# Reordering the setup of a two-layer decoder trunk, and computing the two coarsest tree levels of its decay scores as small tiles

## The chip, the core and the metric

The kernel runs on one core of a Trainium2 chip. The metric is the device time of one execution in microseconds. The kernel was run three times, and the median of the runs is what a change is judged by. One further execution was recorded by the hardware profiler, and all rows shown come from that one.

The engines are called by their profile names: PE is TensorE (PEld its weight loads), ACT is ScalarE, DVE is VectorE, POOL is GpSimd, SP is SyncE, which here only issues the weight transfers.

## What is computed

One inference step of a two-layer trunk with 256 prompt tokens and 8 single-token samples, 264 columns in all, with a model width of 1024. Each layer is a feed-forward block, a mixer and a second feed-forward block. Each block is normalised and modulated by a condition vector (adaLN), and all weights are float32. The mixer has three branches: A and C are gated linear recurrences with 4 heads, B is a convolution with a gated scan.

```python
mod = (c @ w_ada[l] + b_ada[l]).reshape(B, N_SUB, 3, D_MODEL)[:, :, :, None, :]
h = ada_norm(x, norm_gain[l, 0], mod[:, 0, 0], mod[:, 0, 1])
x = x + 0.5 * mod[:, 0, 2] * swiglu(h, w_ffn_in[l, 0], w_ffn_out[l, 0])
h = ada_norm(x, norm_gain[l, 1], mod[:, 1, 0], mod[:, 1, 1])
y, sa, scv, sh, sc = mixer_block(h, ...)
x = x + mod[:, 1, 2] * y
h = ada_norm(x, norm_gain[l, 2], mod[:, 2, 0], mod[:, 2, 1])
x = x + 0.5 * mod[:, 2, 2] * swiglu(h, w_ffn_in[l, 1], w_ffn_out[l, 1])
```

The recurrence of A and C is, per token, S_t = diag(f_t) S_{t-1} + k_t v_t^T and o_t = S_t^T q_t. Written out for the prompt it needs a score for each pair of a query token t and a key token s before it: the product of q_t and k_s, weighted by all decays between them.

## The kernel before

**Weight units.** All matmuls of the trunk run in a sequence of units. A unit is 128x1024 weights. SP loads it into one of six buffers of `raw`; ACT rounds it to `whi` (`split_hi`, line 419); DVE takes the difference as `wlo` (`split_lo`, line 427); PE then runs three matmuls per 128x128 block (`mm3`, lines 462 to 464: high by high, high by low, low by high). `whi` and `wlo` have four slots, and both splits are issued three units ahead (`LOOK`). Per layer there are 44 units for a feed-forward input, 24 for its output, and 82 for the mixer.

**Order by hand.** Each engine walks through the units in one loop and does its own part of the other work at unit numbers written in the tables `AT`, `EARLY_AT`, `HEAD_AT`, `PE_LV` and `RG_AT`. Engines run their queues in order, so a step that waits holds up everything placed behind it. The results of a group of matmuls lie in rotating banks; `take_bank` makes PE wait until the group three before has been evacuated, by ACT or DVE (`BY_ACT`). For the mixer's units 46 to 57 the gate tiles `mb` are evacuated by ACT into `sg`, and the two halves of each `br b` unit by DVE.

**Condition blocks.** `c @ w_ada` is done in blocks of eight tiles of 128x1024 (`ada_units`, line 617), which `to_mod` on DVE transposes and adds to the bias. Two blocks are needed before the first unit: block 0, the scale, is tiles 0 to 7, and block 1, the shift, is tiles 8 to 15. Their tiles go to a buffer `first`; PE waits for them in groups of four. Later blocks run at the units of `plan_ada` and `MIX_ADA`.

**Setup.** PE transposes the inputs, takes tiles 0 to 3, transposes the small parameters (`rows`), takes tiles 4 to 7, sums the squares of x (`add_squares`), takes tiles 8 to 11, spreads the root (`spread_root`), takes tiles 12 to 15 and runs ten matmuls that compute nothing (`keep_warm`, two instructions each). ACT squares x, then runs Exp, Exp and Ln for the gate parameters, then the root of the mean square. DVE copies x and the parameters, does some twenty small operations on the parameters and three on masks, then the reciprocal of the root (line 1664), `to_mod(0)`, the eight scaled tiles (line 2128), `split_lo(0)`, `to_mod(1)` and the low parts of the first eight tiles (line 2140). POOL builds seven level masks from DVE's mask operations.

**Decay tree.** The scores are built in nine levels, `LEVELS = [0, 1, 2, 4, 8, 16, 32, 64, 128]`. At level m a key in the first half of a block of 2m tokens meets a query in its second half, and `update` multiplies q and k by the decays so far. `level` on PE multiplies, for each head and each of two 128-token tiles, all 128 keys with the 64 queries that are in second halves (128x128 weights, 64 columns); `keep` on DVE copies from the bank to `sc` only where the level's mask says so (`copy_predicated`). `PE_LV` places the levels; level 32 of A is at unit 38, level 64 at 43; those of C are at 47 and 50. `keep` and `update` follow one unit later.

**Sample states.** POOL's chain for six batches of states: broadcast v (`outer`, line 1086), multiply with k (line 1092, event `kv`), load the next state batch (`st_load`). ACT scales the loaded state (at `AT['st']`), and DVE adds the product (event `st_new`, at `AT['kv']` + 1), which releases the next `outer`. Then PE multiplies with q (`AT['so']`).

## Time and profile before

| what | value |
| --- | --- |
| median of 3 runs | 1497.16 us (1493.77 to 1501.41) |
| the profiled execution | 1495.62 us |
| its span, first to last instruction | 1493.5 us |
| mean granted clock of PE, share of full speed | 0.996 |
| busy: PE, PEld | 1460.4 us (98%), 1393.4 us (93%) |
| busy: DVE, ACT, POOL | 941.7 us (63%), 779.2 us (52%), 108.8 us (7%) |
| HBM traffic | 215 GB/s over the span |

Busy time of an engine is the time in which it ran an instruction; matmuls are pipelined, so a busy PE isn't PE at its peak. A timeline row gives the start and the length in microseconds, the engine, the line, the operation, the output and inputs with their shapes, a count where rows were merged, and in brackets the idle time before it with what ended that. In a chain view, matmuls and their weight loads are counted once for each pass: a float32 matmul of the kinds here is two instructions.

### The profile page before, as it was taken

Reading aid. Unit: us, or ns where it says so; the run is one execution under the profiler, and the core shown is the slowest. Engines: PE = TensorE matmul, PEld = TensorE weight load, DVE = VectorE, ACT = ScalarE, POOL = GpSimd, SP = SyncE. Lnnn points to the kernel's source line nnn. Section 1 sums busy time; section 2 is a strip of 40 time slices with the busy share of each in tenths; the row PEclk is TensorE's granted clock in tenths of the full one; section 3 lists DMA queues with packets and bytes.
Section 4 is the critical chain, followed back from the end, with each engine's and each line's share of the span. In section 5 each row is a group of like instructions: output and inputs, shape, how many; then the busy total and the mean of one; then the engine's idle time right before and its main releaser. Section 6 shows DMA issues by size and latency. Waiting matters only on the chain.

```text
span 1493.5 us, 30844 instructions
## 1 busy us (share of the span) xinstructions
PE 1460.4 (98%) x12902; PEld 1393.4 (93%) x12902; DVE 941.7 (63%) x1579; ACT 779.2 (52%) x1236; POOL 108.8 (7%) x143
## 2 busy tenths in 40 slices
PE   5999999999999999999999999999999999999998
PEld 4999999999988999999999999999999899999997
DVE  4545546778856677555576545577897667855553
ACT  2534435776446566444464444478643555744442
POOL 3000000012120030000000000000122102000000
PEclk9999999999999999999999999999999999999999
DMA  9689897688787755888957789867889856578661
GB/s 340 193 233 260 239 263 207 191 234 241 210 214 220 211 166 164 247 254 241 260 163 226 226 242 270 231 191 214 242 220 248 234 154 193 164 223 227 181 189 40
DMA packets 460026, 323.59 MB, mean 217 GB/s; under 512 B 11219, under 2 KB 435707, under 8 KB 459890
## 3 DMA queue, kind: packets, MB, share of 16 engines
q1 hardware_dynamic: 451952, 299.44, 70.2%
q0 software_dynamic: 6880, 20.41, 4.9%
q8 instruction: 102, 1.67, 0.5%
q10 hardware_dynamic: 1058, 1.79, 0.3%
q14 instruction: 34, 0.28, 0.1%
HBM read 313.29 MB, written 8.37 MB: 215 GB/s over the span
## 4 chain that ended last, share of the span: by engine, by line
PE 89%; issue 3%; DVE 2%; DMA 2%; POOL 1%; ACT 1%; ACTq 1%; DVEq 0%; POOLq 0%
PE bank L462 27%; PE bank L463 26%; PE bank L464 26%; PE bank L617 4%; PE bank L777 2%; DMA st<-in_state_gla 1%; DMA rows<-in_b_ada 1%; ACT st L1155 1%; POOL xA L1092 1%; DVE wlo L427 0%; PE bank L817 0%; ACTq L1164 0%; DMA raw<-in_w_ada 0%; PE bank L629 0%; PE bank L644 0%
## 5 line engine op out<-in xcount | busy, mean ns | idle before, releaser
L427 DVE TENSOR_TENSOR wlo<-raw,whi 128x1024 fp32r<-128x1024 f32 (+1 forms) x436 | 518.5, 1202 | 386.7 <-ACT whi L419 386.5
L462 PE MATMUL bank<-hH,whi 128*128 128x264 f32 x2048 | 588.9, 288 | 1.9 <-DVE hL L2140 1.4
L463 PE MATMUL bank<-hL,whi 128*128 128x264 f32 x2048 | 580.8, 284 | 0.0
L464 PE MATMUL bank<-hH,wlo 128*128 128x264 f32 x2048 | 580.1, 283 | 0.0
L419 ACT ACTIVATE whi<-raw 128x1024 fp32r<-128x1024 f32 (+1 forms) x436 | 444.2, 1034 | 193.0 <-PE bank L464 152.2
L462 PEld LDWEIGHTS bank<-hH,whi 128*128 128x128 f32 x2048 | 385.8, 188 | 19.9 <-issue 16.5
L463 PEld LDWEIGHTS bank<-hL,whi 128*128 128x128 f32 x2048 | 386.2, 189 | 0.0
L464 PEld LDWEIGHTS bank<-hH,wlo 128*128 128x128 f32 x2048 | 384.4, 188 | 0.0
L462 PE MATMUL bank<-hidH,whi 128*128 128x264 f32 x704 | 201.5, 286 | 0.0
L464 PE MATMUL bank<-hidH,wlo 128*128 128x264 f32 x704 | 200.0, 284 | 0.0
L463 PE MATMUL bank<-hidL,whi 128*128 128x264 f32 x704 | 199.5, 283 | 0.0
L462 PEld LDWEIGHTS bank<-hidH,whi 128*128 128x128 f32 x704 | 132.4, 188 | 2.8 <-issue 2.5
L464 PEld LDWEIGHTS bank<-hidH,wlo 128*128 128x128 f32 x704 | 132.7, 188 | 0.0
L463 PEld LDWEIGHTS bank<-hidL,whi 128*128 128x128 f32 x704 | 132.3, 188 | 0.1
L1155 ACT ACTIVATE hidH<-hid 128x264 fp32r<-128x264 f32 x88 | 37.3, 423 | 148.7 <-DVE hid L1541 148.7
L462 PE MATMUL bank<-uH,whi 128*128 128x274 f32 x320 | 94.4, 295 | 0.0
L463 PE MATMUL bank<-uL,whi 128*128 128x274 f32 x320 | 92.8, 290 | 0.0
L464 PE MATMUL bank<-uH,wlo 128*128 128x274 f32 x320 | 92.5, 289 | 0.0
L1155 ACT ACTIVATE sil<-bank 128x264 f32<-128x264 f32 x76 | 29.7, 391 | 103.0 <-PE bank L464 102.9
L462 PE MATMUL bank<-yH,whi 128*128 128x264 f32 x256 | 74.8, 292 | 6.1 <-ACT sg L1155 3.8
L464 PE MATMUL bank<-yH,wlo 128*128 128x264 f32 x256 | 73.2, 286 | 0.0
L463 PE MATMUL bank<-yL,whi 128*128 128x264 f32 x256 | 73.2, 286 | 0.0
(307 smaller groups left out, 1713.9 us busy)
## 6 DMA issues: line engine op xcount, KB each, us to landing
raw<-in_w_ffn_in SPq DMA_DIRECT2D x176, 512.0 KB, 5.5
raw<-in_w_ada SPq DMA_DIRECT2D x128, 512.0 KB, 4.5
raw<-in_w_in SPq DMA_DIRECT2D x120, 512.0 KB, 5.2
raw<-in_w_ffn_out SPq DMA_DIRECT2D x64, 512.0 KB, 6.3
raw<-in_w_ffn_out SPq DMA_DIRECT2D x32, 384.0 KB, 6.1
first<-in_w_ada SPq DMA_DIRECT2D x16, 512.0 KB, 12.1
raw<-in_w_out SPq DMA_DIRECT2D x16, 512.0 KB, 4.9
out<-st POOLq DMA_DIRECT2D x12, 512.0 KB, 4.6
```

Source lines behind the costliest of these rows:

```text
L419: nc.scalar.activation(whi[:, s, 0:w], raw[:, r, 0:w], ACT.Copy).then_inc(hi_done, 1)
L427: nc.vector.tensor_tensor(wlo[:, s, 0:w], raw[:, r, 0:w], whi[:, s, 0:w].bitcast(F), ALU.subtract).then_inc(lo_done, 1)
L462: nc.tensor.matmul(out, a, rh, start=start, stop=False)
L463: nc.tensor.matmul(out, a, rl, start=False, stop=False)
L464: return nc.tensor.matmul(out, b, rh, start=False, stop=stop)
L617: last = mm(ps[32 * j:32 * j + 32, 0:256].rearrange("p (b i) -> p b i", i=32), cst[:, kt], src[:, j], start=(kt == 0), stop=(kt == KT - 1))
L777: last = mm(out, k_, q_, start=True, stop=True)
L1092: g.tensor_tensor(v_, v_, bc(k_, [P, NB, P]), ALU.mult).then_inc(S["kv"], 1)
L1155: return nc.scalar.activation(out, in_, func, **k)
```

## The change

The setup is reordered. PE waits for the first condition tiles in groups of 6, 5, 4 and 1; it takes tiles 0 to 5, the sums of squares, the parameter transposes, tiles 6 and 7, the spread of the root, then tiles 8 to 15. ACT runs one Sqrt on a dummy ahead of the squares and goes to the root without Exp and Ln. These (`small_act`) move to the first feed-forward stage at unit 13, and DVE's small operations to units 12 (`small_start`) and 15 (`small_end`), the mask operations included; DVE copies the parameters behind the reciprocal. The buffer `setup_t` is moved so that it lives that long.

At levels 32 and 64 of the tree PE multiplies only the keys and queries that belong together: 64x64 scores, or two 32x32 ones, per head and tile, written to their own partitions. DVE copies them without a mask.

The first output unit of the mixer waits for the weights of the second one only when it comes to them. Places of single steps change:

| table entry | before | after |
| --- | --- | --- |
| `MIX_ADA`, last of six | 66 | 63 |
| `AT['kv']`, batch 0 | 22 | 20 |
| `AT['st']`, batch 5 | 48 | 49 |
| `EARLY_AT['conv']`, third tile | 15 | 13 |
| `HEAD_AT['A']['scaled']`, first pair | 56 | 55 |
| `HEAD_AT['C']['spread']`, first pair | 64 | 63 |

The diff without these entries; the removed lines of the small operations, cut here, come back in `small_end`:

```diff
@@ -30,6 +30,8 @@
...
 FIRST = 16
+FIRST_GROUPS = (range(0, 6), range(6, 11), range(11, 15), range(15, 16))
+FIRST_OF = {n: i for i, g in enumerate(FIRST_GROUPS) for n in g}
 UW = NT + 10
@@ -47,7 +49,7 @@
...
 
-MIX_ADA = (10, 16, 29, 44, 53, 66)
+MIX_ADA = (10, 16, 29, 44, 53, 63)
 ADA_BLOCKS = [(0, 1), (0, 0)]
@@ -317,7 +319,7 @@
...
         landed = [sem(f"landed{i}") for i in range(RAW)]
-        first_in = [sem(f"first_in{i}") for i in range(FIRST // 4)]
+        first_in = [sem(f"first_in{i}") for i in range(len(FIRST_GROUPS))]
         hi_done = sem("hi_done")
@@ -512,7 +514,7 @@
...
                 if n < FIRST:
-                    sp.dma_start(first[:, n], src).then_inc(first_in[n // 4], 16)
+                    sp.dma_start(first[:, n], src).then_inc(first_in[FIRST_OF[n]], 16)
                 else:
@@ -607,7 +609,7 @@
...
                     if n < FIRST:
-                        pe.wait_ge(first_in[n // 4], 64)
+                        pe.wait_ge(first_in[FIRST_OF[n]], 16 * len(FIRST_GROUPS[FIRST_OF[n]]))
                         tile = first[:, n, :]
@@ -681,7 +683,7 @@
...
                         if (L, f, k) == (0, 0, 0):
-                            pe.wait_ge(set_dve, 3 + KT + 1 + kt + 1)
+                            pe.wait_ge(set_dve, 2 + KT + 1 + kt + 1)
                         elif k == first and kt % 2 == 0:
@@ -771,6 +773,11 @@
...
                         out = AUX[bank][:, col:col + n]
+                        if m in (32, 64):
+                            for c in range(0, P, 2 * m):
+                                last = mm(AUX[bank][c:c + m, col:col + m], K[br][rows_, j, s0 + c:s0 + c + m],
+                                          Q[br][rows_, j, s0 + c + m:s0 + c + 2 * m], start=True, stop=True)
+                            continue
                         if 0 < m < P:
@@ -905,9 +912,10 @@
...
                     elif j == 0:
-                        unit_ready(pe, n + 1)
                         two = [take_bank()[:, 0:NT] for _ in range(2)]
                         for i, ks_ in ((0, range(6)), (1, range(6)), (0, (6, 7))):
+                            if i:
+                                unit_ready(pe, n + 1)
                             for k in ks_:
@@ -973,20 +981,19 @@
...
 
-            ada_units(0, 4)
+            ada_units(0, 6)
+            pe.wait_ge(set_pool, 3)
+            for k in range(KT):
+                add_squares(0, 0, k)
             pe.wait_ge(set_load[0], 16 * N_ROWS)
...
             last.then_inc(set_pe, 1)
-            ada_units(4, 4)
-            pe.wait_ge(set_pool, 3)
-            for k in range(KT):
-                add_squares(0, 0, k)
-            ada_units(8, 4)
+            ada_units(6, 2)
             spread_root(0, 0)
-            ada_units(12, 4)
+            ada_units(8, 8)
             pe.wait_ge(set_dve, 2)
@@ -1163,16 +1170,21 @@
...
                 act.dma_start(rows[0:72, 2 + l, :], b_ada[l].rearrange("(t p) -> t p", p=P)).then_inc(set_load[0], 16)
+            act.wait_ge(set_pool, 3)
+            a(scrap[:, :], epst[:, :], ACT.Sqrt)
             for k in range(KT):
...
 
-            act.wait_ge(set_dve, 3)
-            a(setup_t[:, 0:2, 0:4], setup_t[:, 0:2, 0:4], ACT.Exp).then_inc(set_act, 1)
-            a(setup_t[:, 4:6, 0:4], setup_t[:, 4:6, 0:4], ACT.Exp).then_inc(set_act, 1)
-            act.wait_ge(set_act, 2)
-            a(setup_t[:, 4:6, 0:4], setup_t[:, 4:6, 0:4], ACT.Ln, bias=1.0).then_inc(set_act, 1)
+            def small_act():
+
+                act.wait_ge(set_dve, 2 + KT + 1 + KT + 1)
+                a(setup_t[:, 0:2, 0:4], setup_t[:, 0:2, 0:4], ACT.Exp).then_inc(set_act, 1)
+                a(setup_t[:, 4:6, 0:4], setup_t[:, 4:6, 0:4], ACT.Exp).then_inc(set_act, 1)
+                act.wait_ge(set_act, KT + 3)
+                a(setup_t[:, 4:6, 0:4], setup_t[:, 4:6, 0:4], ACT.Ln, bias=1.0).then_inc(set_act, 1)
+                nc.scalar.preload_act_table_set("silu_and_others")
 
@@ -1282,6 +1294,8 @@
...
                         split_hi(act, n + LOOK)
+                        if (L, f, k) == (0, 0, 13):
+                            small_act()
                         group_done(act, L, si, k)
@@ -1507,7 +1521,7 @@
...
             wait(act, "mod_ready", 0, 1)
-            dve_tiles = 3
+            dve_tiles = 2
             for k in range(KT):
@@ -1574,43 +1588,43 @@
...
             dve.sem_inc(S["x_ready"], KT)
-            dve.wait_ge(set_pe, 4)
-            st_(v.tensor_copy(par_all[:, :, 0:76], AUX[2][:, 80:232].rearrange("p (l n) -> p l n", l=2)))
-            st_(v.tensor_copy(par_all[:, :, 76:148], AUX[2][:, 240:384].rearrange("p (l n) -> p l n", l=2)))
-
-            for c in (slice(PC["rba"], PC["rbx"] + 4), slice(PC["hnorm"], PC["gnorm"] + 1)):
-                st_(v.tensor_single_scalar(par_all[:, :, c], par_all[:, :, c], 0.5, ALU.mult))
-            dve.sem_inc(set_dve, 1)
-
             both = lambda n: par_all[:, :, PC[n]:PC[n] + 4]
...
             logits = par_all[:, 0, PC["lb"]:PC["lb"] + 4 * NL].rearrange("p (l n) -> p l n", l=NL)
-            st_(tt(s4(2), logits[:, 0], logits[:, 1], ALU.max))
-            st_(tt(s8(0), logits, bc(setup_t[:, 2:3, 0:4], [P, NL, 4]), ALU.subtract))
-            st_(neg_abs(s8(4), both("lam")))
-            dve.sem_inc(set_dve, 1)
-            dve.wait_ge(set_act, 2)
-            st_(tt(s4(2), s4(0), s4(1), ALU.add))
...
-            dve.sem_inc(set_mask, 1)
+
+            def small_start():
+
+                for c in (slice(PC["rba"], PC["rbx"] + 4), slice(PC["hnorm"], PC["gnorm"] + 1)):
+                    st_(v.tensor_single_scalar(par_all[:, :, c], par_all[:, :, c], 0.5, ALU.mult))
+                st_(tt(s4(2), logits[:, 0], logits[:, 1], ALU.max))
+                st_(tt(s8(0), logits, bc(setup_t[:, 2:3, 0:4], [P, NL, 4]), ALU.subtract))
+                st_(neg_abs(s8(4), both("lam")))
+                dve.sem_inc(set_dve, 1)
+
+            def small_end():
+
+                dve.wait_ge(set_act, KT + 3)
+                st_(tt(s4(2), s4(0), s4(1), ALU.add))
+                st_(v.reciprocal(s4(2), s4(2)))
+                st_(tt(s8(0), s8(0), bc(setup_t[:, 2:3, 0:4], [P, NL, 4]), ALU.mult))
+                st_(tt(s4(3), s4(0), s4(1), ALU.add))
+                st_(tt(s4(1), s4(3), s4(0), ALU.subtract))
+                st_(tt(s4(0), s4(0), s4(0), ALU.subtract))
+                st_(ts(both("oml"), s8(0), -1.0, 1.0, ALU.mult, ALU.add))
+                st_(v.tensor_copy(both("low"), s8(0)))
+
+                st_(ts(both("nsp"), both("lam"), -1.0, 0.0, ALU.mult, ALU.max))
+                dve.wait_ge(set_act, KT + 4)
+                st_(tt(both("nsp"), both("nsp"), s8(4), ALU.add))
+                st_(v.tensor_single_scalar(both("nsp"), both("nsp"), -2.0, ALU.mult))
+                st_(v.tensor_single_scalar(both("nsp2"), both("nsp"), 2.0, ALU.mult))
+
+                mi = lambda k: mask[:, k, :].bitcast(I32)
+                st_(tt(mi(2), mi(0), mi(1), ALU.bitwise_xor))
+                st_(tt(mask[:, 3, :], mi(0), mi(1), ALU.is_gt))
+                st_(v.tensor_copy(mask[:, 4, :], mi(2)))
+                dve.sem_inc(set_mask, 1)
 
@@ -1776,6 +1790,10 @@
...
                         low_hidden(pair)
+                    if (L, f, k) == (0, 0, 12):
+                        small_start()
+                    if (L, f, k) == (0, 0, 15):
+                        small_end()
                     ada_ends(L, si, k - 2)
@@ -1879,6 +1897,17 @@
...
                                     AUX[2 + e][:, :].rearrange("p (j t n) -> p j t n", j=2, t=2)[:, :, t])
+                    elif m in (32, 64):
+                        both_t = sc[br][:, :, :].rearrange("p h (t k) -> p t h k", k=P)
+                        for c in range(0, P, 2 * m):
+                            r_, q_ = slice(c, c + m), slice(c + m, c + 2 * m)
+                            for e in (range(1) if br == "A" else range(2)):
+                                if br == "A":
+                                    dst, src = both_t[r_, 0:3:2, :, q_], AUX[0][r_, :].rearrange("p (t h n) -> p t h n", t=2, h=4)
+                                else:
+                                    dst = both_t[r_, 0:3:2, e:4:2, q_]
+                                    src = AUX[2 + e][r_, 0:256].rearrange("p (j t n) -> p t j n", j=2, t=2)
+                                last = v.tensor_copy(dst, src[:, :, :, 0:m])
                     else:
@@ -2119,11 +2148,16 @@
...
             inverse_root(0, 0)
-            normed_samples(0, 0)
+            dve.wait_ge(set_pe, 4)
+            st_(v.tensor_copy(par_all[:, :, 0:76], AUX[2][:, 80:232].rearrange("p (l n) -> p l n", l=2)))
+            st_(v.tensor_copy(par_all[:, :, 76:148], AUX[2][:, 240:384].rearrange("p (l n) -> p l n", l=2)))
+
+            dve.sem_inc(set_dve, 1)
             to_mod(0)
...
             wait(dve, "G_ready", 0, 0)
+            normed_samples(0, 0)
             for k in range(KT):
@@ -2134,13 +2168,13 @@
...
             tt(tmp[:, :, T:NT], tmp[:, :, T:NT], mod[:, 0:8, 1:9], ALU.add).then_inc(set_dve, 1)
-            dve.wait_ge(set_dve, 3 + KT + 1)
+            dve.wait_ge(set_dve, 2 + KT + 1)
             for k in range(KT):
-                dve.wait_ge(set_act, 4 + k + (k > 0))
+                dve.wait_ge(set_act, 1 + k + (k > 0))
                 last = v.scalar_tensor_tensor(hL[:, k, 0:T], tmp[:, k, 0:T], mod[:, k, 0:1], hH[:, k, 0:T].bitcast(F),
...
                 if k == 0:
-                    dve.wait_ge(set_act, 5)
+                    dve.wait_ge(set_act, 2)
                     last = tt(hL[:, :, T:NT], tmp[:, :, T:NT], hH[:, :, T:NT].bitcast(F), ALU.subtract)
```

## Rows read from the trace of the kernel before

**Rows 1.** Busy time by stretch, first mixer: stretch, length, then each engine, clock, DMA.

```profile
265.00:545.00 280.00, 275.22 (x2411) 258.36 (x2411) 207.48 (x350) 165.44 (x271) 44.22 (x51) 0.99 0.75 213
```

**Rows 2.** Timeline of TensorE, setup: start, length, instructions, idle time before and its releaser.

```profile
16.92 3.64 PE L617 MATMUL bank<-first,cst 128*32 128x256 f32 x32
...
24.49 1.91 PE L617 MATMUL bank<-first,cst 128*32 128x256 f32 x32
...
30.44 3.08 PE L617 MATMUL bank<-first,cst 128*32 128x256 f32 x32 [1.12 <-DMA first<-in_w_ada]
...
33.45 5.08 PE L652 MATMUL bank<-ones 128*128 128x256 f32 x20
...
41.64 0.39 PE L462 MATMUL bank<-hH,whi 128*128 128x264 f32 x1 [1.41 <-DVE hL L2140]
```

**Rows 3.** Timeline of ScalarE (ACT) and VectorE (DVE), setup.

```profile
19.29 2.61 ACT L1155 ACTIVATE tmp<-x 128x264 f32<-128x264 f32 x8 [6.56 <-DVEq L1576]
...
24.13 1.28 ACT L1155 ACT_TABLE_LOAD   x1
...
24.15 0.16 DVE L1541 TENSOR_TENSOR setup_t<-setup_t 128x4 f32<-128x4 f32 x1 [0.43 <-ACT setup_t L1155]
...
27.60 0.57 DVE L1664 RECIPROCAL rq<-rq 128x66 f32<-128x66 f32 x1
...
31.02 3.92 DVE L2128 SCALAR_TENSOR_TENSOR tmp<-x,Gs,rstd 128x256 f32<-128x256 f32 x8
...
36.39 0.44 DVE L1620 STREAM_TRANSPOSE adaT<-bank 128x256 f32<-128x256 f32 x1
```

**Rows 4.** DMA issues in progress at 6.1 and 20.8 us; last number: us to landing.

```profile
first<-in_w_ada SPq DMA_DIRECT2D x1, 512.0 KB, 15.8
...
first<-in_w_ada SPq DMA_DIRECT2D x1, 512.0 KB, 7.9
```

**Rows 5.** Busy time by stretch, around the end of the hole in the first mixer.

```profile
443.00:449.00 6.00, 4.87 (x27) 4.87 (x28) 5.17 (x6) 5.97 (x10) 0.90 (x1) 0.72 0.45 120
```

**Rows 6.** Chain that ended last: start, length, engine, output, line, count.

```profile
242.57 0.94 PE bank L629 x56
...
331.81 2.82 PE bank L777 x32
...
375.12 1.04 PE bank L777 x16
```

**Rows 7.** Timeline around the mixers' hole: ScalarE, then TensorE of both mixers.

```profile
440.41 2.45 ACT L1155 ACTIVATE st<-st,bC 128x128 f32<-128x128 f32 x8 [13.25 <-DMA st<-in_state_gla]
...
443.71 0.37 ACT L1155 ACTIVATE sg<-bank 128x264 f32<-128x264 f32 x1
...
445.88 0.38 ACT L1155 ACTIVATE sg<-bank 128x264 f32<-128x264 f32 x1
...
444.13 0.59 PE L462 MATMUL bank<-yH,whi 128*128 128x264 f32 x1 [2.13 <-ACT sg L1155]
...
1169.43 0.39 PE L462 MATMUL bank<-yH,whi 128*128 128x264 f32 x1 [1.70 <-ACT sg L1155]
...
1171.70 0.36 PE L462 MATMUL bank<-hH,whi 128*128 128x264 f32 x1 [0.54 <-ACT sg L1155]
```

**Rows 8.** Timeline of VectorE in the first feed-forward stage: pairs of weight splits.

```profile
87.55 2.36 DVE L427 TENSOR_TENSOR wlo<-raw,whi 128x1024 fp32r<-128x1024 f32 x2 [2.06 <-ACT whi L419]
...
93.35 2.36 DVE L427 TENSOR_TENSOR wlo<-raw,whi 128x1024 fp32r<-128x1024 f32 x2 [2.17 <-ACT whi L419]
```

**Rows 9.** Timeline around unit 21 of the mixer: VectorE, GpSimd (POOL).

```profile
322.47 1.33 DVE L1887 COPY_PREDICATED scA<-mask,bank 128x256 f32<-128x256 int32 x2
...
324.50 2.18 POOL L1092 TENSOR_TENSOR xA<-xA,kA 128x1024 f32<-128x1024 f32 x1 [7.02 <-DMA xA<-v_rows]
```

**Rows 10.** Timeline ahead of the output tiles: VectorE, TensorE.

```profile
530.73 0.41 DVE L1983 SCALAR_TENSOR_TENSOR gA<-XB,bank 128x264 f32<-128x264 f32 x1
...
531.41 0.36 PE L462 MATMUL bank<-yH,whi 128*128 128x264 f32 x1 [1.13 <-POOL yL L1136]
```

24 lines of the change are left out of this document (4 added, 20 removed).

## The prediction

> **What bounds the kernel now.** I read the busy time by stretch first. In the first mixer TensorE (PE) is busy 275.22 of 280 us, so 4.8 us are idle [rows 1], and the second repeats it. Ahead of the main stream, which starts at 38.5 us, it waits for others [rows 2]. Elsewhere it is hardly ever idle but for the last microseconds, which the change doesn't touch. So TensorE is the bound, and the change can pay in three ways only: a main stream that starts earlier, idle holes that go, and fewer microseconds of matmul work in places where no hole behind them takes the gain back. Next I read the setup on each engine [rows 2, 3], the landings [rows 4], the granted clock [rows 5], the price of a decay level [rows 6], the hole in the mixer [rows 7], the rhythm of the feed-forward stage [rows 8], and two places at which work is moved [rows 9, 10].
>
> **Setup: what limits the start.** Two chains meet at 38.5 us. One is the normalisation: the squares end on ScalarE at 21.90 us, but the reciprocal of the root runs on VectorE only at 27.60, since the small parameter work stands ahead of it there and ScalarE has an Exp, a Ln and their table load of 1.28 us in its way; the scaled tiles then run 31.02 to 34.94 [rows 3]. The other chain is the last condition block: tiles 12 to 15 start at 30.44, when the last lands, and take 3.08 us, then ten warming matmuls take 5.08 us and end at 38.53, just as the main stream starts [rows 2].
>
> New first chain: PE takes tiles 0 to 5 from 16.92 on, still at the slow rate of 3.64 us for four [rows 2] for most of it, so until 21.5, and sums the squares right behind (22.2), root 22.6, reciprocal 0.57 [rows 3] to 23.3, tiles 6 and 7 by 23.6, spread 24.7, root copied 25.2, scaled tiles 3.92 us [rows 3], so 29.5 with the small gaps: 5.4 us earlier. Tile 10, which now has to be there before unit 6, was issued at 6.1 and landed 15.8 us later, at 21.9 [rows 4], so it costs nothing. The copy of the parameters, now behind the reciprocal on VectorE, adds 0.6 us, already in that sum.
>
> New second chain: no DMA is issued differently, so tile 14 still lands at 20.8 + 7.9, some 28.6 us [rows 4], and tile 15 at 30.4 [rows 2]. Four tiles take 1.91 us at the full clock [rows 2]: tiles 11 to 14 run 28.6 to 30.5 and tile 15 to 31.0, against 33.5 before. The warming matmuls stay ten. Their 20 instructions cost 5.08 us right behind tiles that ran slowly, at 3.08 for 1.91 [rows 2], so the first of them ran slowly too; for the full clock I take 4.3, bounds 4.1 and 5.08. So the start is 35.3 at best. But PE now idles from about 26.2 to 28.6, a longer hole than the one before 30.44, behind which the four tiles took 3.08 instead of 1.91 [rows 2]. The clock can then fall to its 1.2 GHz level again. Behind the mixer's hole the granted clock means 0.72 over six microseconds, so 3.4 us at half speed, 1.7 lost [rows 5]; with that the start is 37.0. I take the middle, 36.1: **-2.4 us**, bounds -3.2 and -1.0.
> VectorE now reaches the end of this chain ahead of PE. Its first tile pairs no longer hold PE up, and the idle 1.41 us at 41.64 [rows 2] goes: from the transpose at 36.39 [rows 3] to that point it is 5.2 us, so from 31.2 the tile is ready at 36.5, before 36.1 + 1.5. **-1.4 us**, bounds -1.4 and 0.
>
> **Small parameter work, now inside the first feed-forward stage.** ScalarE gets two Exp, one Ln and three table loads of 1.28 [rows 3] at unit 13, 4.4 us, and waits some 1 us first for VectorE; VectorE gets some 1.1 us at unit 12 and 3.3 us at unit 15 (the 16 operations that ran from 24.15 until just before the reciprocal at 27.60 [rows 3]). Behind them in their queues stand the weight splits, for which PE waits with three units in hand. A pair of units takes 5.80 us, the distance of VectorE's pairs of splits, and such a pair 2.36 [rows 8]. Followed through on the old clock: ScalarE is free at 88.5, its splits 17 and 18 end at 91.2, VectorE's at 92.6; PE wants 17 at 91.8 and finds it at 91.5. Then the hidden tile to 94.0, the small end part to 97.3, split 19 to 98.5, wanted at 97.6. **+1.0 us**, bounds 0 (one table load fewer) and +2.5. GpSimd's mask work moves here too, behind it.
> On that last part row and rule differ. In the setup VectorE went through its tiles beside GpSimd's mask operations at 0.49 us each [rows 3], without a gap. The Trainium skill, SBUF — State Buffer, "Who interferes with whom", says that a VectorE instruction with two SBUF inputs contends with a GpSimd one that reads SBUF, and that the loser fully blocks. By it each split could lose a mask operation's length. That would be another 0.6 to 1.2 us at unit 19; I leave it in the upper bound.
>
> **Decay levels 32 and 64.** A level of branch A and one of C together take 2.82 us, C's alone 1.04, so A's is 1.78 in 16 instructions, 0.11 each, though they stream only 64 columns [rows 6]; C's, with 64 weight rows alternating between array halves, need 0.065. So A is held by loading 128 weight columns. With 64 weight columns I take half: 0.9 us, a gain of 0.8. Level 32 doubles the instructions to 32, with 32 weight columns and 32 streamed: the nearest rows are 56 instructions of 32 weight columns in 0.94 us, 0.017 each [rows 6]. Bounds 0.55 us (that price) and 1.7 (0.053 each, half of A's); I take 1.05, a gain of 0.7, between them, since only two column groups alternate and not four. For C the two levels give 0.3 and 0.15, bounds 0.6 and a loss of 0.7. In all four per mixer 1.95. Here a rule speaks against the change. The Trainium skill, TensorEngine Tiling (Array Packing), "Instruction Overhead", gives each matmul some 60 cycles, and "Key Properties" a drain when the tiling mode changes. With 60 cycles at 2.4 GHz for each of the 32 instructions, level 32 would be 0.8 us (an estimate from that page), no loss. The Trainium skill, TensorE: Matmul & The Clock Gate, "Wait — 56ns, not 53.3ns?", knows a sequencer cost of 62 ns per matmul; by it level 32 would take 2.0 us (estimate) and lose. The trace's 0.017 per instruction speaks against both.
> On VectorE the plain copies replace conditional ones of the same element count: no more than 0.1 us per level either way, five units ahead of the next use, 0.
>
> **What of it counts.** Only level 32 of A (unit 38) lies ahead of the mixer's hole with nothing to swallow it: **-0.7 twice, -1.4**. The other three lie in a stretch whose end is set by GpSimd's chain: VectorE's state sum, broadcast of v, product, state load, and ScalarE's scaling of it at unit 48. ScalarE waits 13.25 us there for the load, then scales to 442.8, splits, evacuates sg at 443.71, and PE starts at 444.13 after 2.13 us idle; in the second mixer it is 1.70 [rows 7]. Then comes the slow stretch of 3.4 us [rows 5]. The change puts that scaling one unit later, so sg of unit 49 leaves at 435 and the hole at 444.13 goes. What is late next is sg of unit 50. It left at 445.88 + 0.38 [rows 7], 3.4 us behind the scaling; one split and one sg (1.2 us) are now ahead of the scaling and no longer between, so it leaves at 445.1, and PE can start unit 52 at 445.3, where it did at 446.9. By then PE has been idle for 3.2 us (it ends unit 51 at 442.1, the three saved levels included). If the clock falls again for as long as it did, that costs 1.7, against 0.3 that was left of the old slow stretch. First mixer: -1.6 + 1.4 = -0.2. In the second, unit 52 started at 1171.70 [rows 7] and by the same distances can start at 1170.6; no slow stretch stood there before, so -1.1 + 1.7 = +0.6. I take **+0.4**, bounds +0.6 and -4.
>
> **Moves costed at nothing.** kv of batch 0 moves from unit 23 to 21 on VectorE. GpSimd's product starts at 324.50 and takes 2.18 [rows 9]; VectorE comes to that place at 322.47 [rows 9], so it now waits 3 us, with the level-1 copies, their updates and splits 25 and 26 queued behind it. The convolution tile moved from 15 to 13 lets v's transpose go 1 us earlier. The updates end at 329.7, PE wants them at the level that starts at 331.8 [rows 6]: covered with 1.9 us to spare, where it was 4.4. If that cover goes, the cost is in the third rival. The last ada group moves from unit 66 to 63 with its loads, SP's queue three units earlier, the same 1.9 us of PE. C's spread at unit 63 needs a reciprocal that ends 1.1 us before. A's scaling at 55 follows a spread by then done. The later wait for the second output weights removes nothing: PE's idle 1.13 us at 531.41 ends 0.27 us behind VectorE's evacuation of 530.73 + 0.41, whose bank the second output tile takes before any matmul [rows 10]; that weight split ended at 527.4.
>
> **Sum.** -2.4 - 1.4 + 1.0 - 1.4 + 0.4 = **-3.8 us**. The profiled execution took 1495.62 (span 1493.5), so 1491.8. That execution is 1.5 us below the median of the three runs, 1497.16, which reach from 1493.77 to 1501.41; against the median it would be 1493.4. I give 1492.0.
>
> **Rivals.**
> (1) The hole at unit 52 doesn't form or is short: the load lands sooner, or ScalarE's order costs less. For it: 4.8 us of idle time per mixer and the slow clock behind it are real [rows 1, 5]. Against: the load chain isn't shortened by any edit. All level savings then count (3.9 in place of 1.4), the holes of 2.1 and 1.7 go with the slow stretch of 1.7: 1495.6 - 2.4 - 1.4 + 1.0 - 3.9 - 5.5 = 1483.4; half of it 1487.
> (2) The start stays where it is, since both the landing of tile 15 and ten warming matmuls remain: slow clock for all of it, 37.5, and the small work costs 1 to 2 us in the stage: 1495.
> (3) Slower: at unit 21 VectorE waits for GpSimd's product longer than 1.9 us beyond my 3. It decides from there: if the broadcast lands 3 us later than here, PE idles 1.1 in front of level 2 and, with a lowered clock, loses 1.7 more, and the updates behind it slip as well, some 4 to 6 per mixer: 1495.6 - 3.8 + 10 = 1501.8.
> (4) The small tiles cost per instruction and not per column. At the 0.065 us that C's instructions now take [rows 6], level 32 is 2.1 us in A, a loss of 0.3 where I have a gain of 0.7: 1491.8 + 2.0, so 1494. For it: C's price is above what 64 columns explain. Against: the 0.017. The skill's 62 ns, named above, would do this.
>
> **Chances.** Forecast 0.45, (1) 0.25, (2) 0.15, (3) 0.07, (4) 0.08. Range: (1) halfway down and (3) halfway up are in, 1485.5 to 1498.0. A change of 0.5%, 7.5 us, is about what a measurement of this kernel can tell from none. Faster by more needs most of (1): 0.25; slower by more needs more than (3): 0.04; within 0.71.
>
> **What would show it.** Main stream's first matmul at 35.3 to 37.0 and no idle at its fifth tile; a hole of about 1 us near unit 19; level 64 of A 0.9 us and level 32 1.05; no hole in the middle of unit 51, one of about 3 us in front of unit 52; 1.1 us still idle in front of the output tiles. The prediction is wrong if the start doesn't move, if the hole in the mixer vanishes, or if VectorE's wait at unit 21 reaches PE.

## The result

The changed kernel takes 1487.73 us (median of 5 runs, 1487.27 to 1489.91), the kernel before 1497.61 in the same comparison; the ratio is 0.9939, 95% interval 0.9918 to 0.9961. The profiled execution took 1487.42 us: 8.2 less than the 1495.62 before, where I had forecast 3.8. The time of 1492.0 was 4.3 too high, and the result lies in the range.

The page of the changed kernel:

```profile
span 1485.4 us, 30971 instructions
...
PE 1453.3 (98%) x12966; PEld 1387.5 (93%) x12966; DVE 936.7 (63%) x1573; ACT 779.8 (52%) x1238; POOL 115.0 (8%) x143
```

PE works 7.1 us less than before, and the span is 8.1 shorter: the gain is matmul time, and the idle time has mostly moved. The starts of level 16 of A (unit 33) and of the first output tile of the mixer, rows with the same idle time before them in both kernels, cut the span into stages. Start to first level: 3.4 us gained. First mixer, from that level to the output tiles: 161.68 to 158.99, 2.7 gained. From there to the second mixer: 0.6 lost. Second mixer: 160.48 to 157.86, 2.6 gained. Behind it: nothing. The rows that cut the first mixer, level 16 of A before and after, then the first output tile after (the one before is in [rows 10]):

```profile
369.73 2.00 PE L777 MATMUL bank<-qA,kA 128*128 128x64 f32 x16 [1.38 <-DVE xA L1541]
...
366.32 2.00 PE L784 MATMUL bank<-qA,kA 128*128 128x64 f32 x16 [1.38 <-DVE xA L1555]
...
525.31 0.36 PE L464 MATMUL bank<-yH,whi 128*128 128x264 f32 x1 [1.12 <-POOL yL L1143]
```

**Setup.** Timeline of PE, then ACT and DVE, of the changed kernel (to compare with [rows 2, 3]):

```profile
17.23 4.66 PE L619 MATMUL bank<-first,cst 128*32 128x256 f32 x48
...
25.18 1.50 PE L619 MATMUL bank<-first,cst 128*32 128x256 f32 x24
...
29.59 2.37 PE L619 MATMUL bank<-first,cst 128*32 128x256 f32 x40 [2.91 <-DMA first<-in_w_ada]
...
31.89 4.58 PE L654 MATMUL bank<-ones 128*128 128x256 f32 x20
...
36.12 0.47 PE L464 MATMUL bank<-hH,whi 128*128 128x264 f32 x1
```

```profile
22.88 0.32 ACT L1162 ACTIVATE rq<-bank,epst 128x66 f32<-128x66 f32 x1 [0.66 <-PE bank L631]
...
23.23 0.57 DVE L1678 RECIPROCAL rq<-rq 128x66 f32<-128x66 f32 x1 [3.72 <-ACT rq L1162]
...
25.93 3.25 DVE L2162 SCALAR_TENSOR_TENSOR tmp<-x,Gs,rstd 128x256 f32<-128x256 f32 x8
...
32.03 0.45 DVE L1634 STREAM_TRANSPOSE adaT<-bank 128x256 f32<-128x256 f32 x1 [1.58 <-PE bank L619]
```

The reciprocal comes 4.4 us earlier and the scaled tiles start at 25.93 instead of 31.02. PE idles 2.91 us before tile 11, yet the last five tiles take 2.37 us, 0.059 per instruction: the rate of the fast four tiles in [rows 2], 1.91 for 32. The granted clock is 1.00 from 30 to 36 us. The main stream starts at 36.1 and never waits for a tile of the first eight.

**Small parameter work.** ACT, DVE and PE in the first feed-forward stage:

```profile
81.87 1.28 ACT L1187 ACT_TABLE_LOAD   x1
...
83.16 0.43 ACT L1162 ACTIVATE hidH<-hid 128x264 fp32r<-128x264 f32 x1
...
91.83 2.63 DVE L429 TENSOR_TENSOR wlo<-raw,whi 128x1024 fp32r<-128x1024 f32 x2
...
101.35 0.64 PE L619 MATMUL bank<-raw,cst 128*32 128x256 f32 x8 [0.47 <-DMA raw<-in_w_ada]
```

ACT is held for 4.4 us (78.73 to 83.16) and DVE for 3.3, as forecast, and PE runs through from 73.1 to 99.4. The only idle time is 0.47 us at a condition tile whose load is late.

**Levels.** Chain that ended last (levels 32 and 64 of A and C, to compare with [rows 6]), the other two from the timeline:

```profile
385.79 0.60 PE bank L778 x30
...
437.68 0.61 PE bank L778 x16
...
403.49 1.15 PE L778 MATMUL bank<-qA,kA 128*64 128x64 f32 x16
...
420.38 0.46 PE L778 MATMUL bank<-qC,kC 64*32 64x32 f32 x32
```

**The mixers' hole.** ACT's scaling of state batches 4 and 5, PE behind them in both mixers, and a stretch with the granted clock in the third column from the end ([rows 5, 7] before):

```profile
416.76 2.45 ACT L1162 ACTIVATE st<-st,bC 128x128 f32<-128x128 f32 x8 [7.56 <-DMA st<-in_state_gla]
...
436.49 2.45 ACT L1162 ACTIVATE st<-st,bC 128x128 f32<-128x128 f32 x8 [1.28 <-DMA st<-in_state_gla]
...
422.66 0.67 PE L846 MATMUL bank<-st,qs 64*32 64x256 f32 x16 [1.82 <-ACT sg L1162]
...
429.03 0.67 PE L805 MATMUL bank<-scA,VTA 128*128 128x256 f32 x2 [1.06 <-DVE vC L1979]
...
1150.31 0.67 PE L805 MATMUL bank<-scA,VTA 128*128 128x256 f32 x2 [1.83 <-DVE vC L1979]
...
423.00:428.00 5.00, 4.96 (x40) 4.50 (x24) 4.93 (x8) 0.82 (x1) 0.95 (x2) 0.66 1.01 270
```

There is no hole at unit 51 and none in front of unit 52. In the first mixer ACT now waits 7.56 us for the load of batch 4, where it waited 3.87 before; splits and evacuations pile up behind it, and PE idles at units 47 and 48 with the clock at 0.66 in between. The second mixer idles 1.83 at unit 48, and the clock is 0.72 from 1150 to 1156 us.

### The profile page after: what moved, and what is told of

Its sections match the earlier page's. It is cut to its first block, busy times and chain, and to the rows that moved or that the text cites. A ratio compares the mean times of both kernels' runs of the same rounds, so it can differ in the third digit from the quotient of the medians.

```text
span 1485.4 us, 30971 instructions
## 1 busy us (share of the span) xinstructions
PE 1453.3 (98%) x12966; PEld 1387.5 (93%) x12966; DVE 936.7 (63%) x1573; ACT 779.8 (52%) x1238; POOL 115.0 (8%) x143
## 3 DMA queue, kind: packets, MB, share of 16 engines
q10 hardware_dynamic: 1058, 1.79, 0.3%
## 4 chain that ended last, share of the span: by engine, by line
PE 90%; DVE 3%; DMA 2%; issue 2%; ACT 1%; SPq 1%; POOL 1%; DVEq 0%; ACTq 0%; POOLq 0%
PE bank L464 27%; PE bank L465 26%; PE bank L466 26%; PE bank L619 4%; PE bank L784 2%; SPq L517 1%; DVE wlo L429 1%; DMA st<-in_state_gla 1%; DMA first<-in_w_ada 1%; PE bank L805 1%; DMA raw<-in_w_ada 1%; PE bank L824 0%; ACT whi L421 0%; PE bank L631 0%; POOL yL L1143 0%
## 5 line engine op out<-in xcount | busy, mean ns | idle before, releaser
L1162 ACT ACTIVATE sil<-bank 128x264 f32<-128x264 f32 x76 | 29.6, 390 | 97.9 <-PE bank L466 97.9
```

The source lines that it names most:

```text
L1162: return nc.scalar.activation(out, in_, func, **k)
```

## Experiments

Each kernel was compared with the kernel before on its chip. "Before" there had medians of 1497.15 to 1498.3, and single executions of one kernel spread by some 10 us, so I read the ratio with its interval, and the trace for where the time is.

**1. The small tiles alone.** The kernel before, with the diff's parts in `level` and `keep` and nothing else.

> The kernel before with only the small score tiles of levels 32 and 64, on TensorE and VectorE; setup, tables and waits stay as before. Theory A (my prediction's prices): the four levels save 1.95 us per mixer, but only level 32 of A lies ahead of the hole at unit 51, so 0.7 per mixer is kept and the hole grows from 2.1 and 1.7 us by the rest: -1.4 us in all. Theory B (read from the trace of the changed kernel, where the levels cost 1.08, 0.60, 0.61 and 0.42): 2.9 us are saved per mixer, 1.1 of it ahead of the hole; if the state load stays where it is, about -1.1 per mixer, -2.3 in all, and the hole at unit 51 grows to 3.5 to 4 us. Theory C: the load comes earlier too, since VectorE and ScalarE reach the earlier states sooner; then up to -5.8 us in all.

Measured: 1495.03, ratio 0.9984 (0.997 to 0.9999), 2.1 us under the median of before. The trace shows the new hole of the changed kernel, and a small rest of the old one:

```profile
421.36 2.46 ACT L1160 ACTIVATE st<-st,bC 128x128 f32<-128x128 f32 x8 [7.91 <-DMA st<-in_state_gla]
...
427.26 0.67 PE L844 MATMUL bank<-st,qs 64*32 64x256 f32 x16 [2.17 <-ACT sg L1160]
```

So the total is near theory B's 2.3 us, though A's 1.4 lies within the interval too; C's 5.8 doesn't. B's picture is wrong: the hole does not grow at unit 51. It moves to units 47 and 48. PE arrives there earlier, and the load of batch 4 lands later: it takes 8.5 us from the end of its product to the scaling, against 5.2 in the kernel before.

**2. The setup alone.**

> The kernel before with only the new order of the setup and the small parameter work in the first feed-forward stage. Theory A (prediction): -2.4 (start) -1.4 (fifth tile) +1.0 (hole near unit 19) = -2.8 us, if the mixers' hole doesn't absorb it. Theory B (read from the changed kernel): start at 36.1 to 36.4 and no hole but one of under 0.5 us at a condition tile: -3.4 us at the start of the first mixer. In both the second mixer and all else are unchanged; if the state load chain of the first mixer is tied to the engines and not to the clock on the wall, the whole of it arrives at the end.

Measured: 1494.12, ratio 0.9974 (0.9959 to 0.999), 3.0 us under before. The interval covers both theories; in the trace the main stream starts at 36.0, and the level of unit 33 stands 3.6 us earlier, nearer to B's 3.4. In the profiled execution the second mixer lost this again: the load of batch 4 was late there (ACT waits 7.03 us, PE 4.14 at unit 48).

**3. The moved entries alone.**

```diff
-'kv': (22, 26, 36, 41, 44, 48) ... 'st': (14, 17, 33, 37, 44, 48)
+'kv': (20, 26, 36, 41, 44, 48) ... 'st': (14, 17, 33, 37, 44, 49)
```

with the other four entries and the later `unit_ready`.

> The kernel before with only the moved table entries (kv of batch 0 two units earlier, the scaling of the last state batch one unit later, third convolution tile, last condition group, two head entries) and the later wait for the second output weights; levels as masked 128-wide products, setup as before. Theory A (prediction): the holes of 2.13 and 1.70 us at unit 51 become holes in front of unit 52 of about 1.2 to 1.6 us less what the saved levels would have added: -0.5 to -1.5 per mixer, with the clock low behind them: 0 to -2 us in all. Theory B (what sets the hole is only that the scaling stands ahead of sg of unit 49): no hole is left in units 50 to 52, -3.8 us and another -1.7 for the slow clock of the first mixer, -5.5 in all.

Measured: 1499.04, ratio 1.0002 (0.9987 to 1.0018), no gain. PE in both mixers:

```profile
448.35 0.36 PE L462 MATMUL bank<-hH,whi 128*128 128x264 f32 x1 [2.85 <-ACT sg L1156]
...
1173.95 0.36 PE L462 MATMUL bank<-hH,whi 128*128 128x264 f32 x1 [2.32 <-ACT sg L1156]
```

This is the hole that I had forecast, in front of unit 52, 2.85 and 2.32 us long. Scaling one unit later only moves it: theory A holds for the place, and B falls. A's lengths of 1.2 to 1.6 us were too short.

The three parts alone have ratios whose product is 0.996, and the changed kernel has 0.9939. The intervals don't tell whether the parts help one another.

**4. The scaling back at unit 48.**

> The changed kernel with one table entry put back: the scaling of the last state batch on ScalarE at unit 48 as before, not at 49. Theory A (the move of the scaling is what removed the hole at unit 51): the hole returns with 2 us or more in each mixer, with slow clock behind it: +3 to +6 us against the changed kernel. Theory B (the state load itself came earlier, 436.4 us in place of 440.4 while TensorE was only 5.5 us earlier, and TensorE had already waited 2.9 us at units 47 and 48): ScalarE sends sg of unit 49 at 440.3, TensorE wants its bank at 441.1, no hole: 0 to +1 us.

Measured: 1490.72, ratio 0.9953 (0.9935 to 0.9971), 3 us above the changed kernel, with overlapping intervals. The first mixer has its hole at unit 51 again (1.84 us) and yet takes 158.64 us, no more than the 158.99 of the changed kernel. Batch 4's load was less late there (ACT waits 4.41 us for it, PE 1.38 at unit 48), and the granted clock stays at 1.00. In the second mixer it was late (ACT waits 7.50), PE idles 1.76 and 4.33 us at units 47 and 48, and the mixer takes 162.8. Neither theory is right as put: where the hole stands depends on the entry, how long it is depends on the loads.

**5. Both state loads earlier.** GpSimd's queue:

```diff
-                outer(L, 4)
                 st_load(L, 4)
+                outer(L, 4)
                 st_store(L, 3)
-                outer(L, 5)
                 st_load(L, 5)
+                outer(L, 5)
```

> The changed kernel with one more edit: GpSimd issues the loads of state batches 4 and 5 ahead of the broadcast and product of the same batch, not behind them (some 8 us earlier). Theory A (the holes in the mixer come from the landing of these two loads, for which ScalarE waits with splits and evacuations queued behind it): ScalarE no longer waits at units 44 and 49, the holes of 1.82, 1.06 and 1.83 us go and with them the slow clock behind them (1.8 us each): 4.5 us in the first mixer, 3.5 in the second, -8 us against the changed kernel, about 1479.7. Theory B (VectorE and the product of GpSimd are just as late): the wait goes over to the add of the product, at most -3 us. Theory C (the earlier loads collide with weight transfers that are short there, DMA busy 90% and more): a new wait for weights, 0 or slower.

Measured: 1479.58, ratio 0.9885 (0.9867 to 0.9902), 8.2 us under the changed kernel. ACT no longer waits:

```profile
408.83 2.44 ACT L1162 ACTIVATE st<-st,bC 128x128 f32<-128x128 f32 x8
...
430.08 2.44 ACT L1162 ACTIVATE st<-st,bC 128x128 f32<-128x128 f32 x8
```

No hole is left between unit 33 and the output tiles in either mixer; they take 154.14 and 155.69 us. The total is theory A's to the microsecond. Its parts are not: the mixers gained 4.9 and 2.2 us where A had 4.5 and 3.5, and in the profiled execution about 1 us came from outside them.

**6. The same edit on the kernel before.**

> The kernel before with only the earlier issue of the loads of state batches 4 and 5. Theory A (the load is what ScalarE waits for, and all of the mixers' idle time at unit 51 with its slow stretch comes from that): -3.8 us for the holes of 2.13 and 1.70 and -1.7 for the slow clock, so -5 to -6 us. If so, the changed kernel with the same edit and this one differ by setup and level tiles alone: 3.4 + 5.8 = 9.2 us. Theory B (the product is as late as the load, 8.7 us of broadcast and product from VectorE's last add): a hole of 1 us or more stays at unit 51.

Measured: 1491.45, ratio 0.9955 (0.9939 to 0.9971), 6.4 us under before; no hole in the mixers, 157.40 and 158.98 us. Against experiment 5 this prices the levels, with the moves, where no hole falsifies them: 3.26 and 3.29 us per mixer. I had forecast 1.95. The levels' own rows give 2.7 (1.13 + 0.6 + 0.6 + 0.4). I had expected 9.2 us between the two kernels; it is 11.9 by the medians and 10.5 by the traces, 3.8 of it up to the level of unit 33.

**7. The small tiles four times.**

```diff
-                            for c in range(0, P, 2 * m):
+                            for c in [c for _ in range(4) for c in range(0, P, 2 * m)]:
```

> The changed kernel with each small score tile of levels 32 and 64 computed four times (the same result each time), to price the instructions themselves. If an instruction costs what its weight columns cost (0.07 us for 64 columns and 0.018 for 32 in branch A, 0.038 and 0.014 in C, from the trace of the changed kernel), the levels take about 4.5, 2.3, 2.3 and 1.7 us instead of 1.1, 0.6, 0.6 and 0.4: +8.0 us per mixer. If a fixed cost per instruction or a drain between forms made up most of the level (my rival with 0.065 us each), level 32 of A would be 8 us in the fourfold form; if most of the 0.6 us is the start and end of the level, the added instructions cost less than 0.01 each.

Chain that ended last, levels 32 and 64 of A, then of C (some records are missing; 128 and 64 instructions were issued at each level 32 and 64):

```profile
389.50 2.11 PE bank L778 x125
...
408.79 3.88 PE bank L778 x64
...
428.48 1.52 PE bank L778 x110
...
445.20 2.62 PE bank L778 x64
```

Per instruction issued that is 0.017 and 0.061 in A, 0.012 and 0.041 in C; the single ones cost nearly the same (0.019 and 0.072; 0.014 and 0.038). By the difference between the two kernels, 0.1 us of a level 32 and 0.2 of level 64 of A doesn't grow with the instructions. So there is no large start or end of a level; the price hangs on the weight columns. The single execution took 1498.97 us. Its first mixer is 7.3 us longer than in the changed kernel, near the 8.0 expected, its second 3.8: there the idle time at unit 48 is gone, so the added work seems to have filled it.

**8. Tiles of 32 keys by 16 queries at levels 1 to 16,** with the early loads; DVE's masked copies stay as they are.

```diff
+                        if 0 < m < 32 and br in 'AC':
+                            for c in range(0, P, 32):
+                                last = mm(AUX[bank][c:c + 32, col + c // 2:col + c // 2 + 16].rearrange("p (n m) -> p n m", m=m),
+                                          K[br][rows_, j, s0 + c:s0 + c + 32],
+                                          Q[br][rows_, j, s0 + c:s0 + c + 32].rearrange("p (n two m) -> p n two m", two=2, m=m)[:, :, 1],
+                                          start=True, stop=True)
+                            continue
```

> The changed kernel with the earlier state loads and, at levels 1 to 16, tiles of 32 keys by 16 queries (four per head and 128 tokens) in place of 128 keys by 64 queries; VectorE's masked copies stay. By the price per instruction of level 32 (0.018 in A, 0.014 in C) a level of A takes 1.15 us instead of 1.73 and one of C 0.9 instead of 1.04: 0.6 and 0.1, five levels each, 3.5 us per mixer. Theory A: all of it arrives, -7 us against the same kernel without the fine tiles. Theory B: VectorE, for whose update TensorE already waits 1.38 us at unit 33, takes part of it back: -3 to -5 us. Theory C: four column groups in turn cost 0.065 each as 64-row weights do: slower by 20 us.

Measured: 1469.05, ratio 0.9815 (0.9795 to 0.9836), 10.5 us under experiment 5. A level of C, then one of A with PE's wait for VectorE in front:

```profile
352.22 0.66 PE bank L778 x48
...
1076.98 0.74 PE L778 MATMUL bank<-qA,kA 128*32 128x16 f32 x64 [1.37 <-DVE xA L1562]
```

64 instructions of 32 weight columns in four column groups take 0.66 to 0.74 us (the chain's rows have lost some records), 0.010 each, in A and in C. That is cheaper than my price from two groups, and the gain is more than theory A's 7 us. By the rows 1.07 and 0.38 are saved per level, 14.5 us in all. 4 of them don't arrive: in the profiled execution 1.8 are a later main stream (37.6 for 35.8, see experiment 11), and PE has new idle times of 0.3 to 0.8 us for VectorE's state adds and one of 1.06 for a condition tile.

**9. Only batch 4's load earlier.**

> The changed kernel with the earlier issue of the load of state batch 4 alone; that of batch 5 stays behind its product. Theory A (the load of batch 4 landed late in the changed kernel and by that took the place of the hole that I had predicted in front of unit 52): the idle times at units 47 and 48 go (1.82 + 1.06, 1.83, with their slow clock, 8 us in both mixers), TensorE reaches unit 52 with nothing lost before, and the predicted hole of about 3 us stands there in both mixers, with slow clock behind it: +4 to +5 us each; in all 0 to +2 us against the changed kernel, 1488 to 1490. Theory B (the load of batch 5 is early enough once batch 4 is on time): no hole, 1480 as with both loads early.

Measured: 1487.37, ratio 0.9922 (0.9899 to 0.9945), the changed kernel's time. The first mixer shows theory A: the predicted hole stands in front of unit 52, 1.95 us long. There is one of 0.99 at unit 48 too, of another kind:

```profile
440.02 0.36 PE L464 MATMUL bank<-hH,whi 128*128 128x264 f32 x1 [1.95 <-ACT sg L1162]
...
423.54 1.89 POOL L1099 TENSOR_TENSOR xA<-xA,kC 128x1024 f32<-128x1024 f32 x1 [7.12 <-DMA xA<-v_rows]
...
424.01 1.53 DVE L1979 TENSOR_SCALAR vC<-soT 128x8 f32<-128x8 f32 x2
...
425.68 0.67 PE L805 MATMUL bank<-scA,VTA 128*128 128x256 f32 x2 [0.99 <-DVE vC L1979]
```

The two small DVE operations take 1.53 us beside GpSimd's product, and 0.24 in the changed kernel, where they ran before it. In the second mixer no hole is left at unit 52, as theory B has it, since batch 5's load came with ACT waiting just 1.45. Both loads have to be early for the gain.

**10. The moves costed at nothing, put back.**

> The changed kernel with all moves that the prediction costed at nothing put back: kv of batch 0 at unit 22, convolution tile at 15, last condition group at 66, the two head entries, and the wait for the second output weights in front of the first output tile. Theory A (prediction): 0, within 1 us of 1487.7; VectorE's wait of 1.79 us for GpSimd at unit 21 goes, TensorE doesn't see it; idle 1.13 us in front of the output tiles as before. Theory B (one of them carries part of the gain that I had not forecast, 4.4 us): +2 us or more.

Measured: 1492.12, ratio 0.9955 (0.9937 to 0.9973), with a spread of 1486.74 to 1495.78. The profiled execution is the fastest of them and no slower than the changed kernel; it shows nothing that these entries cost. Whether the median is really higher stays open, the intervals overlap.

**11. Six warming matmuls in the idle time before tile 11,** on kernel 8.

```diff
-            ada_units(8, 8)
+            ada_units(8, 3)
             pe.wait_ge(set_dve, 2)
-            keep_warm(WARM)
+            keep_warm(6)
+            ada_units(11, 5)
+            keep_warm(9)
```

> The kernel with early state loads and fine tiles, with six warming matmuls in TensorE's idle time in front of condition tile 11 and nine instead of ten behind tile 15. In six executions of the new setup TensorE idled 2.19, 2.46 and 2.91 us there with the clock at full speed behind it and the main stream at 35.8 to 36.1 us, and 3.36, 3.39 and 3.68 us with the clock at 0.72 to 0.81 and the main stream at 37.4 to 37.7. Theory A (the idle time is what lets the clock fall): full clock in every execution, main stream at 35.7 to 36.0, so 1 to 1.7 us off the kernel without it when that fell in the slow case, 0 in the other; about 1468 against 1469.05. Theory B (the slow matmuls come from contention with the transfers in this stretch, not from the clock): tiles 11 to 15 still take over 3 us in some executions, and the six added matmuls are lost time: 0 or slower.

Measured: 1470.23, ratio 0.9805 (0.978 to 0.983): no gain. What the setup did, in kernel 8 and here:

```profile
29.45 3.30 PE L619 MATMUL bank<-first,cst 128*32 128x256 f32 x40 [3.36 <-DMA first<-in_w_ada]
...
30.00:36.00 6.00, 6.00 (x48) 3.93 (x41) 2.72 (x8) 2.45 (x6) 0.00 (x0) 0.72 1.12 287
...
27.40 2.86 PE L654 MATMUL bank<-ones 128*128 128x256 f32 x12
...
30.19 2.37 PE L619 MATMUL bank<-first,cst 128*32 128x256 f32 x40
...
30.00:36.00 6.00, 6.00 (x58) 4.32 (x57) 3.95 (x10) 2.62 (x6) 0.00 (x0) 1.00 1.18 290
```

The clock does stay at 1.00, and in experiment 12 too. That fits theory A, but it did so in five of eight executions without the added matmuls as well, so two don't show that the idle time is what lets it fall. The main stream starts at 36.3 instead of 37.6. But PE then waits 1.77 us for a condition tile until 103.51, where kernel 8 waited 0.39 until 102.77: in this execution the 1.3 us are gone by there. That this is so in all of them isn't shown.

**12. Level 0 of A as 32 by 32 tiles on the diagonal as well,** on kernel 11.

```diff
+                        if m == 0 and br == "A":
+                            for c in range(0, P, 32):
+                                last = mm(AUX[bank][c:c + 32, col + c:col + c + 32], K[br][rows_, j, s0 + c:s0 + c + 32],
+                                          Q[br][rows_, j, s0 + c:s0 + c + 32], start=True, stop=True)
+                            continue
```

> As the kernel with warming matmuls in the gap, and level 0 of branch A also as 32 by 32 tiles on the diagonal (64 instructions of 32 weight columns in place of 16 of 128; VectorE's masked copy stays). By the prices so far, 0.0104 for 16 streamed columns in four column groups and 0.017 for 32 in two groups, the level takes 0.7 to 1.1 us instead of 1.78: -1.4 to -2.2 us for both mixers, if nothing behind it takes that back. The stage behind it already waits for VectorE's adds at the first states in the fine kernel (0.78 us), so the rival is 0.

Measured: 1467.14, ratio 0.9792 (0.9769 to 0.9815), 3.1 us under kernel 11, whose interval (0.978 to 0.983) overlaps this one.

```profile
306.46 0.69 PE bank L778 x50
```

The level takes 0.69 in place of 1.78, 2.2 us for both mixers; the rest of the 3.1 has no row here. It streams twice the columns of the fine levels at the same price. This kernel has the lowest median of all, 2.1% under the kernel before.

## Why the prediction was right, and where its steps failed

**Right by range and in kind, wrong in size.** The measured gain is over twice the forecast. By its own signs the prediction was part wrong: the hole in front of unit 52 and that near unit 19 are missing. The mixers' term missed by 4.3 us, and with it the time; the other misses cancel. The terms:

| term | forecast, us | measured, us |
| --- | --- | --- |
| start of the main stream | -2.4 | -2.4 in this execution, -0.8 to -2.8 in others |
| fifth tile | -1.4 | -1.4 |
| small work in the first stage | +1.0 | +0.5, elsewhere |
| levels, both mixers | -3.9 | -5.5 by the rows, -6.6 by the mixers without holes |
| holes of the mixers | +2.9, so the mixers -1.0 | moved; the mixers -5.3 |
| between the mixers | 0 | +0.6, of it 0.37 idle at a condition tile |
| moves | 0 | 0 by rows, median open |

**Start.** 36.1 was the mean of two cases, and both exist, so to hit it was luck. In the eight profiled executions that have the new setup and not the warming matmuls of experiment 11, tiles 11 to 15 ran at full clock behind 2.1 to 2.9 us of idle time, with the main stream at 35.7 to 36.1 (the changed kernel and experiments 2, 5, 9 and 10), and slowly behind 3.4 to 3.7 us, with it at 37.4 to 37.7 (4, 7 and 8). Without slow clock I had 35.3; the 0.8 between is the later landing of tiles 11 to 14, at 29.6 for my 28.6. Experiments 1 and 3, which have the old setup, show which chain had to be shortened: there tiles 12 to 15 ran in 1.94 and 1.93 us, and yet the main stream started at 39.33 and 38.73, after 2.39 and 1.76 us of waiting for VectorE.

**Small work.** The step that failed is ScalarE's time: I had it free at 88.5 on the old clock, but it was free at 83.16, which is 87.0 there. The microsecond of waiting for VectorE didn't arise, since `small_start` had run in front of it. The first split of the pair at 91.83 ended at about 93.1; PE, with a unit every 2.93 us from 73.1 on, wanted it for unit 19 at 93.6. The cover is thin. The Trainium skill, SBUF — State Buffer, "Who interferes with whom", would have VectorE's splits and GpSimd's masks contend. The pairs of splits took 2.63 and 2.45 for 2.36 [rows 8], while GpSimd's seven mask operations took 6.49 where they took 4.56 before: the row agrees that they contend, and most of the loss fell on GpSimd, where nobody waits. The row that the prediction set against the rule, eight scaled tiles in 3.92 us [rows 3], held contention too: with the mask operations gone from beside them the same eight take 3.25 us in every trace with the new setup, and 3.92 in every one with the old.

**Levels.** The mis-sized term. Level 32 of A took 0.60 for my 1.05, C's 0.46 and 0.61 for 0.74 and 0.89; only level 64 of A was dearer, 1.08 to 1.15 for 0.9. I set the prices in the middle between 0.017 and half of A's 0.11. Experiment 7 shows that 0.017 was the right row, though only two column groups alternate here. Rival (4) falls with it. So does the estimate by the Trainium skill, TensorEngine Tiling (Array Packing), "Instruction Overhead": 60 cycles at 2.4 GHz are 0.025 us for each instruction, and experiment 8 shows 0.010. The 62 ns that the prediction has from the Trainium skill, TensorE: Matmul & The Clock Gate, "Wait — 56ns, not 53.3ns?", stand there for matmuls with hardware decode off; no run here shows which way they were decoded, and 0.010 us is far below them. The drain that the same page's "Key Properties" tells of has no row of its own here; by experiment 7 it can be no more than the 0.1 us of a level 32 that doesn't grow with the instructions.

**The hole.** The step "the load chain isn't shortened by any edit" failed, and with it the place of the hole. Its mechanism was right: experiment 3 shows the hole in front of unit 52, at 2.85 and 2.32 us, and without any gain. What I missed is batch 4, one step up the same chain. With the levels shorter PE, and with it the weight transfers, runs ahead of that load. And the load took longer: its two transfers 5.8 us in the changed kernel and 4.2 before:

```profile
st<-in_state_gla POOLq DMA_DIRECT2D x2, 256.0 KB, 5.8
...
st<-in_state_gla POOLq DMA_DIRECT2D x2, 256.0 KB, 4.2
```

That the shorter levels make it longer isn't shown. Experiment 1 has 6.1 us with the levels alone, but experiment 2, with the old levels, has 4.4 in its first mixer and 5.8 in its second, and only there the hole at unit 48. PE then stands at units 47 and 48, and GpSimd waits 5.35 us for the next broadcast in place of 7.65. So batch 5 is in time, and the hole that I had forecast doesn't form: one hole took the place of the other. Why the broadcast came sooner is argued only: while PE stands, fewer weights are asked for. That the holes come from these loads is shown by experiments 5 and 6; which transfer delays them is not, and stays open. Rival (1) was half right: the hole at unit 52 was gone and the levels counted, but the idle time wasn't.

**Moves.** At unit 21 VectorE waits 1.79 us for GpSimd (forecast: 3), and PE doesn't see it. What I hadn't seen is that the splits behind it now run beside GpSimd's next product:

```profile
320.94 1.23 DVE L1555 TENSOR_TENSOR st<-st,xA 128x1024 f32<-128x1024 f32 x1 [1.79 <-POOL xA L1099]
...
326.00 5.20 DVE L429 TENSOR_TENSOR wlo<-raw,whi 128x1024 fp32r<-128x1024 f32 x3 [0.28 <-ACT whi L421]
...
326.47 2.51 POOL L1099 TENSOR_TENSOR xA<-xA,kA 128x1024 f32<-128x1024 f32 x1 [3.42 <-DMA xA<-v_rows]
```

Three splits take 5.20 us, where a pair takes 2.36 [rows 8]; the middle one alone takes 2.84. There is room for it. Rival (3) didn't occur. The 1.13 us in front of the output tiles stayed, as forecast.

## What to carry to other kernels

When work on the bounding engine gets shorter, follow the whole chain of transfers and not only the step that was late in the old trace: the step before it may take its place. A load whose target buffer is free belongs ahead of the waits of its queue, not behind them: here that was worth 8.2 us for two lines moved. Before a product is made to fit one large tile, price it as several small ones in different column groups; the work that masks throw away costs its weight columns.

## What the runs showed of the hardware

Float32 matmuls with few weight columns are cheap: in branch A 0.108 us per instruction with 128 of them (1.73 us for 16), 0.061 to 0.072 with 64 that don't alternate, 0.017 to 0.019 with 32 that alternate between two column groups, 0.010 with 32 over four, whether they stream 16 or 32 columns. Per weight column that is 0.84, about 1, some 0.55 and 0.33 ns.

The clock behind PE's idle time in the setup differed between executions of nearly the same code, with idle times that differ by under 2 us: 1.00 behind 2.1 to 2.9 us, 0.72 to 0.81 behind 3.4 to 3.7. The last idle time alone doesn't decide: in the kernel before it was 1.12 us, after another of 1.81, and tiles 12 to 15 still ran slowly (3.08 for 1.91 us, [rows 2]). Filled with matmuls that compute nothing it stayed at 1.00 in both kernels profiled.

Two small DVE operations lost 1.3 us beside a GpSimd product (1.53 for 0.24) and so held PE without being long themselves. A weight split of 1.22 us took 2.84 beside one.
